# A hybrid decoder block on one core: the norm's row spread through memory, the router's scaling moved, two weight pieces moved behind a store

## The chip, the cores and the metric

The kernel runs on one core of one Trainium2 chip. The metric is the device time of one execution in microseconds (us), here the median of a few runs; lower is better. The engines are named as in the profile: PE (TensorE; PEld are its weight loads), DVE (VectorE), ACT (ScalarE), POOL (GpSimd) and SP (SyncE, here only an issuer of DMAs). SPq, ACTq and POOLq are the instruction streams that issue DMAs.

## The reference

All data is float32: 2048 tokens, width 1024, one layer. Cut to what matters:

```python
hn = rms_norm(x, norm_mix)                    # x * rsqrt(mean(x*x) + eps) * gain
proj = hn @ w_in + b_in                       # q k v o, gates i f (4 heads of 128), conv b c x
h_m = mlstm_chunkwise(q * 128**-0.5, k, v, log_i, log_f)
y_m = sigmoid(o) * h_m
y_c = short_gated_conv(cb, cc, cx, conv_w)    # width 3
x = x + concat([y_m, y_c]) @ w_out
hn2 = rms_norm(x, norm_ffn)
moe = hier_moe(hn2, ...)                      # top-1 of 4 groups, top-2 of its 8 experts, 512 wide
out = rms_norm(x + moe, norm_final)           # silu(hn2 @ w_gate[e]) * (hn2 @ w_up[e]) @ w_down[e]
```

## The kernel before

**Stages.** The tokens pass in four blocks (`NB = 4`) of 512 (`TB`), each of four tiles of 128 (`CT`), in the order of the code; then the 32 experts follow, ordered by the number of tokens that chose them. Each engine has its own instruction stream, written out by hand; semaphores (`S_("name")`) tie the streams together. An engine waits in order: all that stands behind a waiting instruction waits too.

**A block.** PE multiplies the transposed, normed input `hnT` with slices of `w_in`, in "parts" of a Strassen-like scheme (seven half-size products in place of eight), first q and k, then the output gate, then the values v (`v_part`, read by DVE in `v_reads`), and the convolution channels between the four chunks of the mLSTM. DVE forms the sums that such products need (`x_sums`, `ysums`), POOL those of the weights (`weight_sums`). The output projection follows as two halves `p` of seven parts each (`out_part`, in the order 1, 7, 6, 2, 5, 3, 4); DVE adds their results and the residual in `out_reads`. In block 0 the value products are read between 85 and 113 us.

**The norm of the next block.** ACT squares and sums the rows of the next block (`norm_squares`), POOL makes `ssx[:, 2, :]`, 128 partitions x 4 tiles, of 1/rms (`norm_scales`, semaphore `rs_ready`). `hnT` has its tokens along the free axis, so 1/rms is needed as one row of 512 tokens on all 128 partitions. Before, DVE multiplied the identity by the four columns (`norm_diagonals`, line 1941, tile `zz`, seen as `rdiag`), and PE multiplied a matrix of ones by it into the PSUM tile `RB` (`norm_rows`, line 812) between the two halves of the output projection; `norm_scaled` (line 1948) multiplied `hnT` by it. Block 0 has a path of its own at the start, which stays as it is.

**The tail of a block on ACT.** After `norm_squares(b + 1)` ACT issues the store of the first tile of x (`store_residual(0)`, line 1332), squares it (line 1340) and goes on with the other tiles. The stored x is loaded again by SP in quads (line 518) and turned by DVE (`turned_tile`, line 2271) for the router's logits on PE (`router_logits`, line 866), which stand behind part 6 of the second half.

**The router's weights.** `wrt` (8 x 64 columns) is multiplied by the norm's gain on DVE once, in block 0, ahead of the sums of y (line 2549); `ysums(0, (1, 2))` follow (lines 2447 and 2450), and PE's part 6 waits for the second.

**From the blocks to the experts.** The rows `hn2` are stored by ACT, the last 128 of them at line 1448. POOL then gathers each expert's tokens from memory: the first 128 of item 0 (line 1719), the up to 32 further ones of item 0 (`gather_tail(0)`, line 1743), then item 1's. The gather of item 0's first rows doesn't need the last stored rows, the tail gather does. Gate and up weights of an expert come as four pieces of 1 MB into `wo`'s place (`gate_up_piece`, line 634), the down weights as two of 1 MB (`down_piece`, line 638: into `og` and `vx`); `first_weights` issues those of item 0. PE needs piece j from its k tile 2j on (`first_gate_up`, lines 1085 and 1087), then does the further rows (`late_gate_up`, line 1118), turns item 1's rows (line 1063), and multiplies by the down weights (line 1157). DVE meanwhile sorts the experts and makes all the indices in one long chain of small dependent operations (lines 2748 to 2843), in which it also turns item 0's further rows (line 2711) and multiplies item 1's hidden rows (`hidden(1)`, line 2705), for which PE's down products wait.

Of the kernel before, what the change touches and what calls it, by code (L numbers as in the profile page):

```python
# [18 lines left out]
P = 128  # L19
# [14 lines left out]
def build(nc, x, xT_d, w_slots, channel_d, bias_d, w_out, w_router, late_d, gfin_d, w_gu, w_dn, out):  # L34
# [35 lines left out]
    wv_d = nc.dram_tensor("w_v_sums", (4, P, KT // 2 * WC), F32, kind="Internal").ap()  # L70
    yn_d = nc.dram_tensor("attention_rows", (S, DM), F32, kind="Internal").ap()
    row3_d = nc.dram_tensor("gate_rows", (H * TB,), F32, kind="Internal").ap()
    slots_d = nc.dram_tensor("slots", (CAP * NE, 2), F32, kind="Internal").ap()
    over_d = nc.dram_tensor("over_slots", (OVMAX * CAP + P, 2), F32, kind="Internal").ap()

    with ExitStack() as ctx:
# [382 lines left out]
        def v_loaded(b, i):  # L459
# [4 lines left out]
            return S_("second_loaded1"), (2 * b + (1 if i == 2 else 2)) * 16  # L464
        NCONST = 2
        NRC = 15 + 2 * TQ
# [17 lines left out]
        def own_instruction(eng):  # L484

            eng.sem_inc(S_("waits_done"), 1)
# [5 lines left out]
        def _(sp):  # L492
# [148 lines left out]
            def first_weights():  # L641
                sp.wait_ge(S_("yn_ready"), NTILE)
                down_piece(0, 0)
                sp.wait_ge(S_("out_part_done"), out_part_end(NB - 1, 1, 7))
                gate_up_piece(0, 0)
                sp.wait_ge(S_("out_part_done"), out_part_end(NB - 1, 1, 4))
                sp.wait_ge(S_("x_gathered"), 16)
                for j in range(1, NWS):
                    gate_up_piece(0, j)
                sp.wait_ge(S_("x4_gathered"), 16)  # L650
                down_piece(0, 1)
# [45 lines left out]
        def _(pe):  # L697
# [111 lines left out]

            def norm_rows(b):  # L810
                pe.wait_ge(S_("rdiag_ready"), b + 1)
                pe.matmul(RB[:], ones[:], zz[:], start=True, stop=True
                          ).then_inc(S_("norm_rows_done"), 1)
# [4 lines left out]
            def first_gates():  # L818

                for k in range(KT):  # L820
                    pe.wait_ge(S_("xg_ready"), k + 1)
                    if k == 0:
                        pe.wait_ge(S_("w_first_loaded"), 16)
                    if k == KH:
                        w_here(0, 4)
                    for t in range(CT):
                        mm = pe.matmul(FIRST_BANK[t][:, 0:WC], xraw[:, k, t * P:(t + 1) * P], slot_weights(4, k, 0, WC),
                                       start=(k == 0), stop=(k == KT - 1))
                        if k == KT - 1:
                            mm.then_inc(S_("proj_done"), 1)  # L830
                w_here(0, 5)
                for t in range(CT):
                    if t >= 2:
                        pe.wait_ge(S_("bank_emptied"), t - 1)
                    for k in range(KT):
                        mm = pe.matmul(FIRST_BANK[CT + t][:, 0:WG], xraw[:, k, t * P:(t + 1) * P],
                                       slot_weights(5, k, 0, WG), start=(k == 0), stop=(k == KT - 1))
                    mm.then_inc(S_("proj_done"), 1)
                    if t == 0:
                        pe.wait_ge(S_("masks_ready"), 1)  # L840
                        norm_rows(0)

# [17 lines left out]
            def router_logits(g, t):  # L860
                pe.wait_ge(S_("wrt_ready"), 1)
                pe.wait_ge(S_("hn2T_ready"), 2 * g + 2)
# [7 lines left out]
            def router_rows(g):  # L870

                pe.wait_ge(S_("both_halves_ready"), 1)
                pe.wait_ge(S_("lgT_ready"), g + 1)
                pe.matmul(STA[:, 0, P:P + NR], lgT[:], both_halves[:], start=True, stop=True
                          ).then_inc(S_("logits_done"), 1)
# [34 lines left out]
            for b in range(NB):  # L910
# [93 lines left out]
                for p in range(2):  # L1004
                    pe.wait_ge(S_("yT_ready"), b * CT + 2 * (p + 1))
                    if p == 1 and b < NB - 1:
                        norm_rows(b + 1)
                    for i, bank, new in OUT_PARTS:
# [213 lines left out]
        def _(act):  # L1222
# [26 lines left out]
            with act.Fori(0, NB) as b:  # L1249
# [76 lines left out]
                with act.If(b < NB - 1):  # L1326
                    norm_squares(b + 1)
                def store_residual(t):
                    g = b * CT + t
# [142 lines left out]
        def _(pool):  # L1472
# [21 lines left out]
            pool.memset(cmask[:].rearrange("h (c t) -> h c t", c=CT)[:, :, 0:1], 0.0).then_inc(m, 1)  # L1494
            pool.wait_ge(m, 15)
            pool.sem_inc(S_("masks_ready"), 1)
            rc = S_("route_consts")
# [439 lines left out]
        def _(dve):  # L1937
            def norm_diagonals(b):
                dve.wait_ge(S_("rs_ready"), b + 1)
                for t in range(CT):  # L1940
# [3 lines left out]
            def norm_scaled(b, half):  # L1944
                dve.wait_ge(S_("norm_rows_done"), b + 1)
                dve.wait_ge(S_(f"xT_loaded{half}"), 16 * (b + 1))
                for k in range(4 * half, 4 * half + 4):
                    dve.scalar_tensor_tensor(out=hnT[:, k, :], in0=hnT[:, k, :], scalar=gmix[:, k:k + 1], in1=RB[:],
                                             op0=ALU.mult, op1=ALU.mult).then_inc(S_("hnT_ready"), 1)
# [14 lines left out]
            for j in range(4):  # L1964
                dve.wait_ge(S_(XRAW_LOADED[j]), 16)
                for k in (2 * j, 2 * j + 1):
                    dve.tensor_scalar(xraw[:, k, :], xraw[:, k, :], gmix[:, k:k + 1], None, ALU.mult
                                      ).then_inc(S_("xg_ready"), 1)
            dve.wait_ge(S_("masks_ready"), 1)
            norm_diagonals(0)  # L1970
            dve.wait_ge(S_("biases_loaded"), 16)
# [50 lines left out]
            class Route:  # L2022
# [126 lines left out]
                def one_hot(self):  # L2149
                    for j in range(2):  # L2150
# [4 lines left out]
                        if j == 0 and self.T == TL:  # L2155
# [5 lines left out]
            dve.tensor_tensor(both_halves[:], ident[:, 0:NR], ident[:, RW:RW + NR], ALU.add  # L2161
                              ).then_inc(S_("both_halves_ready"), 1)
            dve.wait_ge(S_("route_consts"), NRC)
            dve.scalar_tensor_tensor(out=pad[:, 1:2], in0=jcol[:], scalar=-float(R1), in1=pad[:, 0:1], op0=ALU.mult,
                                     op1=ALU.add).then_inc(S_("pad_step"), 1)
            dve.wait_ge(S_("pad_step"), 1)
            dve.tensor_scalar(pad[:, 1:2], pad[:, 1:2], float(P), None, ALU.add).then_inc(S_("pad_step"), 1)
            dve.wait_ge(S_("pad_step"), 2)
            dve.tensor_scalar(mtail[:, 0:1], pad[:, 1:2], float(S + 1 + P + R2), None, ALU.is_lt
                              ).then_inc(S_("pad_step"), 1)  # L2170
            dve.tensor_scalar(mtail[:, 2:3], pad[:, 1:2], float(S + 1 + P + R3), None, ALU.is_lt
                              ).then_inc(S_("pad_step"), 1)
            dve.tensor_scalar(mtail[:, 3:4], pad[:, 1:2], float(S + 1 + P + R4), None, ALU.is_lt
                              ).then_inc(S_("pad_step"), 1)
            dve.tensor_scalar(mtail[:, 1:2], pad[:, 1:2], -1.0, None, ALU.add).then_inc(S_("pad_step"), 1)
            dve.wait_ge(S_("pad_step"), 6)
            dve.tensor_scalar(mtail[:, 1:2], mtail[:, 1:2], float(TQ), jcol[:, 0:1], ALU.mult, ALU.add
                              ).then_inc(S_("pad_step"), 1)
            dve.wait_ge(S_("pad_step"), 7)

            it = S_("item_step")
            item_steps = [0]

            def then(ins):
                item_steps[0] += 1
                ins.then_inc(it, 1)
                dve.wait_ge(it, item_steps[0])


            def decoded(rows_, code, n_, pad_, after):  # L2190
# [9 lines left out]
            for b in range(NB):  # L2200
# [74 lines left out]
                for r in range(RQ):  # L2275
# [14 lines left out]
                    if b > 0:  # L2290
# [19 lines left out]
                        if r == 13:  # L2310
                            routed.slots()
                            dve.sem_inc(rt, NSTEP - routed.n)

                def v_reads(names):

# [32 lines left out]
                if b < 1:  # L2348
                    dve.tensor_tensor(bvd[:], bvo[:, 0, WC:2 * WC], bvo[:, 0, 0:WC], ALU.subtract
                                      ).then_inc(S_("v_bias_ready"), 1)  # L2350
                dve.wait_ge(S_("v_bias_ready"), 1)
                if b > 0:
                    for s in range(2):
                        for t in range(CT):
                            ps = done(number[("o", (s, t))])
                            if s == 1:
                                dve.tensor_tensor(gt[:, t, :], ps[:, WC:WG], bgt, ALU.add
                                                  ).then_inc(S_("gates_ready"), 1)
                            dve.tensor_tensor(og[:, t, s * WC:(s + 1) * WC], ps[:, 0:WC], bvo[:, 1, s * WC:(s + 1) * WC],
                                              ALU.add).then_inc(E, 1)  # L2360
                v_reads(("p1",))
                gates_later((0, 0), (1, 0), (0, 1))

# [181 lines left out]

                dve.wait_ge(S_("consts_loaded"), 16 * NCONST)
                if b < 1:
                    for k in range(KT):
                        i_ = dve.tensor_scalar(wrt[:, k, :], wrt[:, k, :], gffn_c[:, k:k + 1], None, ALU.mult)
                    i_.then_inc(S_("wrt_ready"), 1)  # L2550
                def out_reads(p, names):
# [61 lines left out]
                out_reads(0, ("u2", "c11", "u4", "c22", "r12"))  # L2613
                if b < NB - 1:
                    norm_diagonals(b + 1)
                out_reads(0, ("c12", "u3", "r21", "r22", "c21"))
# [442 lines left out]
```

## Time and profile before

| | |
|---|---|
| median of 3 runs | 1774.49 us (1774.33 to 1776.5) |
| the profiled execution's time | 1775.47 us |
| its span in the profile | 1773.7 us |
| PE busy | 1753.0 us, 99% of the span |
| PEld busy | 1403.6 us, 79% |
| DVE busy | 926.6 us, 52% |
| ACT busy | 234.4 us, 13% |
| POOL busy | 676.3 us, 38% |
| mean granted clock of PE | 0.998 of full speed |

The busy times are of the one profiled execution; its time is 1.8 us above its span. A fp32 matmul stands in the trace as two records. Records of PE overlap in the trace, so the pace of a run of them is the distance of their starts. A row with a bracket names the idle time of the engine ahead of the instruction and what ended it; an "x8" behind a row means that so many instructions are merged in it. Times in the timeline count from the start of the span.

### The profile page before, as it was taken

How to read it: one execution, taken by the hardware profiler on the slowest of the kernel's cores; microseconds unless marked ns; L12 is line 12 of the kernel's file. 1: busy time of each engine (PE TensorE's matmuls, PEld its weight loads, DVE VectorE, ACT ScalarE, POOL GpSimd, SP SyncE). 2: the span in 40 equal slices, each digit the busy share in tenths (PEclk: the TensorE clock that was granted, in tenths of full speed). 3: DMA queues.
4: the chain of work that ended last, by engine and by line, in shares of the span. 5: the costliest groups of instructions: out<-in, count | busy, mean ns of one | idle time of the engine just before them, and what ended most of it. 6: DMA issues, size and time to landing. Idle time of an engine off the chain costs nothing. (4 is left out here: it accounts for less than half of the span.)

```text
span 1773.7 us, 27565 instructions
## 1 busy us (share of the span) xinstructions
PE 1753.0 (99%) x10077; PEld 1403.6 (79%) x10077; DVE 926.6 (52%) x1897; ACT 234.4 (13%) x618; POOL 676.3 (38%) x755
## 2 busy tenths in 40 slices
PE   9999999999999999999999999999999999999997
PEld 8889658889578887588885678887888888888876
DVE  5556785377773677763776683433433233233332
ACT  2021110211101211102210210011110011100111
POOL 5933212044221235030341124444445455554552
PEclk9999999999999999999999999999999999999999
DMA  7553742234732327422334488898999998999984
GB/s 295 222 200 99 273 166 86 96 135 152 258 107 84 131 96 258 163 102 96 129 113 150 167 320 334 336 340 333 347 345 333 353 355 324 348 340 332 346 330 179
DMA packets 101373, 406.81 MB, mean 229 GB/s; under 512 B 20982, under 2 KB 35630, under 8 KB 68464
## 3 DMA queue, kind: packets, MB, share of 16 engines
q1 hardware_dynamic: 57488, 316.78, 48.3%
q0 software_dynamic: 26880, 58.91, 9.3%
q10 hardware_dynamic: 16880, 29.43, 4.5%
q8 instruction: 82, 1.34, 0.3%
q14 instruction: 43, 0.35, 0.1%
HBM read 366.59 MB, written 64.53 MB: 243 GB/s over the span
## 5 line engine op out<-in xcount | busy, mean ns | idle before, releaser
L1135 PE MATMUL ps_proj<-hnT,wo 128*128 128x128 f32 (+4 forms) x992 | 199.9, 283 | 0.0
L1137 PE MATMUL ps_proj<-hnT,wo 128*128 128x128 f32 (+4 forms) x992 | 197.9, 281 | 0.0
L1726 POOL DMA_INDIRECT xin<-hn_rows,idx_quad x116 | 117.3, 1011 | 125.7 <-DVE hnT L2711 46.4
L1135 PEld LDWEIGHTS ps_proj<-hnT,wo 128*128 128x128 f32 x992 | 153.9, 191 | 13.6 <-issue 13.6
L1137 PEld LDWEIGHTS ps_proj<-hnT,wo 128*128 128x128 f32 x992 | 153.2, 191 | 0.0
L743 PE MATMUL ps_proj<-hnT,ww 128*128 128x256 f32 x640 | 151.9, 380 | 0.0
L743 PEld LDWEIGHTS ps_proj<-hnT,ww 128*128 128x128 f32 x640 | 120.1, 191 | 16.4 <-issue 1.4
L1565 POOL TENSOR_TENSOR xres<-ww 128x512 f32<-128x512 f32 x12 | 15.2, 1268 | 291.2 <-DMA ww<-in_w_slots 279.3
L2942 DVE SCALAR_TENSOR_TENSOR hn<-xin,rsy,ww 128x1024 f32<-128x1024 f32 x30 | 38.5, 1285 | 136.1 <-POOL rsy L1784 136.1
L1135 PE MATMUL ps_scores<-hnT,wo 128*128 128x128 f32 (+4 forms) x496 | 99.1, 282 | 0.0
L1135 PE MATMUL ps_rows<-hnT,wo 128*128 128x128 f32 (+4 forms) x496 | 99.0, 281 | 0.0
L1137 PE MATMUL ps_scores<-hnT,wo 128*128 128x128 f32 (+4 forms) x496 | 99.0, 281 | 0.0
L1137 PE MATMUL ps_rows<-hnT,wo 128*128 128x128 f32 (+4 forms) x496 | 98.9, 281 | 0.0
L772 PE MATMUL ps_proj<-wo,yT 128*128 128x512 f32 x192 | 88.8, 600 | 0.0
L2705 DVE TENSOR_TENSOR kT<-qT,ps_proj 128x128 f32<-128x128 f32 (+4 forms) x62 | 15.6, 293 | 134.8 <-ACT qT L1420 134.5
L784 PE MATMUL ps_proj<-ww,hnT 128*128 128x256 f32 (+1 forms) x384 | 84.7, 383 | 0.0
L784 PEld LDWEIGHTS ps_proj<-ww,hnT 128*128 128x128 f32 x384 | 73.1, 190 | 11.0
L1137 PEld LDWEIGHTS ps_scores<-hnT,wo 128*128 128x128 f32 x496 | 76.7, 192 | 0.0
L1135 PEld LDWEIGHTS ps_rows<-hnT,wo 128*128 128x128 f32 x496 | 76.6, 191 | 0.0
L1137 PEld LDWEIGHTS ps_rows<-hnT,wo 128*128 128x128 f32 x496 | 76.6, 191 | 0.0
L1135 PEld LDWEIGHTS ps_scores<-hnT,wo 128*128 128x128 f32 x496 | 76.5, 191 | 0.0
L743 PE MATMUL ps_proj<-xin,ww 128*128 128x256 f32 x320 | 76.4, 381 | 0.0
(523 smaller groups left out, 3493.9 us busy)
## 6 DMA issues: line engine op xcount, KB each, us to landing
wo<-in_w_gu SPq DMA_DIRECT2D x128, 1024.0 KB, 7.7
ww<-in_w_slots SPq DMA_DIRECT2D x43, 1024.0 KB, 4.9
og<-in_w_dn SPq DMA_DIRECT2D x32, 1024.0 KB, 5.3
vx<-in_w_dn SPq DMA_DIRECT2D x32, 1024.0 KB
xin<-in_x SPq DMA_DIRECT2D x16, 512.0 KB, 5.3
ww<-w_v_sums SPq DMA_DIRECT2D x16, 512.0 KB, 3.4
xres<-in_x SPq DMA_DIRECT2D x16, 512.0 KB, 6.1
x_rows<-x ACTq DMA_DIRECT2D x16, 512.0 KB, 3.6
```

The source lines that it names most:

```text
L743: mm = pe.matmul(place, w_(k), x_[:, k, :], start=(new and k == 0), stop=(k == KH - 1), skip_group_check=True)
L772: mm = pe.matmul(place, y_[:, k, :], w_[:, k, :], start=(new and k == 0), stop=(k == KH - 1), skip_group_check=True)
L784: mm = pe.matmul(PROJ[:, n % 2, 0:w], hnT[:, k, t * P:(t + 1) * P], slot_weights(slot, k, 0, w), start=(k == 0), stop=(k == KT - 1))
L1135: pe.matmul(GU[m][:, 0:n_], wo[:, kt, m * P:(m + 1) * P], xT[:, kt, 0:n_], start=(kt == 0), stop=(kt == KT - 1), skip_group_check=True)
L1137: mm = pe.matmul(GU[m][:, CAP:CAP + n_], wo[:, kt, FF + m * P:FF + (m + 1) * P], xT[:, kt, 0:n_], start=False, stop=(kt == KT - 1), skip_g ...
L1565: pool.tensor_tensor(wsum(s, 1, first), a21, a22, ALU.add).then_inc(ready, 1)
L1726: pool.indirect_dma_start(xg[:, t * TC:(t + 1) * TC], None, hn2_d.rearrange("s (j c) -> (s j) c", j=TQ), bass.IndirectOffsetOnAxis(ap=idx_ ...
L2705: i_ = dve.tensor_tensor(hT[:, m, 0:n_], sgt[:, m, 0:n_], src[:, CAP:CAP + n_], ALU.mult)
L2942: dve.scalar_tensor_tensor(out=fo, in0=yr[:], scalar=rsy[:, 1, 0:1], in1=gfin, op0=ALU.mult, op1=ALU.mult).then_inc(S_("out_rows_ready"), 1)
```

## The change

Three things are changed, and some semaphores with them.

1. In blocks 1 to 3 the row of 1/rms no longer comes from PE. ACT waits for POOL's scales, stores the 128 x 4 words in token order in memory (`norm_scales`, 2 KB), waits until they have landed, and loads the row into `zz` on all 128 partitions (256 KB); `norm_scaled` reads `zz`. The products of `norm_rows` and DVE's `norm_diagonals` stay for block 0 alone.
2. The eight scalings of `wrt` stand among DVE's reads of the value products of block 0 (three ahead of the first, five behind it), not ahead of the sums of y.
3. The last gate/up piece and the second down piece of item 0 are issued when the last rows' store has landed. Before, piece 3 was issued when the first gather had landed, the down piece when the tail gather had. What SP issues behind them (`gfin`) moves with them.

Four semaphores are dropped or merged: `masks_ready` (now `mask_step` at 15), `wrt_ready` and `both_halves_ready` (now `router_consts` at 3), `pad_step` and `v_bias_ready` (now the counter of `then`, which waits after each instruction).

```diff
+    scale_d = nc.dram_tensor("norm_scales", (S,), F32, kind="Internal").ap()
...
-                for j in range(1, NWS):
-                    gate_up_piece(0, j)
-                sp.wait_ge(S_("x4_gathered"), 16)
+                gate_up_piece(0, 1)
+                gate_up_piece(0, 2)
+                sp.wait_ge(S_("hn2_stored1"), 16 * NTILE // 2)
+                gate_up_piece(0, 3)
                 down_piece(0, 1)
...
             def router_logits(g, t):
-                pe.wait_ge(S_("wrt_ready"), 1)
+                pe.wait_ge(S_("router_consts"), 3)
...
                 for p in range(2):
                     pe.wait_ge(S_("yT_ready"), b * CT + 2 * (p + 1))
-                    if p == 1 and b < NB - 1:
-                        norm_rows(b + 1)
...
                 with act.If(b < NB - 1):
                     norm_squares(b + 1)
+                    act.wait_ge(S_("rs_ready"), b + 2)
+                    own_instruction(act)
+                    row = scale_d[bass.ds(b * TB, TB)]
+                    act.dma_start(row.rearrange("(t p) -> p t", p=P), ssx[:, 2, :],
+                                  allow_slow_non_contiguous=True).then_inc(S_("scales_stored"), 16)
+                    act.wait_ge(S_("scales_stored"), 16 * (b + 1))
+                    own_instruction(act)
+                    act.dma_start(zz[:], row.partition_broadcast(P)).then_inc(S_("scales_spread"), 16)
...
             def norm_scaled(b, half):
-                dve.wait_ge(S_("norm_rows_done"), b + 1)
+                dve.wait_ge(S_("scales_spread"), 16 * b)
                 dve.wait_ge(S_(f"xT_loaded{half}"), 16 * (b + 1))
                 for k in range(4 * half, 4 * half + 4):
-                    dve.scalar_tensor_tensor(out=hnT[:, k, :], in0=hnT[:, k, :], scalar=gmix[:, k:k + 1], in1=RB[:],
+                    dve.scalar_tensor_tensor(out=hnT[:, k, :], in0=hnT[:, k, :], scalar=gmix[:, k:k + 1], in1=zz[:],
...
+                def router_weights(ks):
+                    if b < 1:
+                        dve.wait_ge(S_("consts_loaded"), 16 * NCONST)
+                        for k in ks:
+                            i_ = dve.tensor_scalar(wrt[:, k, :], wrt[:, k, :], gffn_c[:, k:k + 1], None, ALU.mult)
+                        i_.then_inc(S_("router_consts"), 1)
...
+                router_weights(range(3))
                 v_reads(("p1",))
+                router_weights(range(3, KT))
                 gates_later((0, 0), (1, 0), (0, 1))
...
-                dve.wait_ge(S_("consts_loaded"), 16 * NCONST)
-                if b < 1:
-                    for k in range(KT):
-                        i_ = dve.tensor_scalar(wrt[:, k, :], wrt[:, k, :], gffn_c[:, k:k + 1], None, ALU.mult)
-                    i_.then_inc(S_("wrt_ready"), 1)
...
                 out_reads(0, ("u2", "c11", "u4", "c22", "r12"))
-                if b < NB - 1:
-                    norm_diagonals(b + 1)
                 out_reads(0, ("c12", "u3", "r21", "r22", "c21"))
```

## Rows read from the trace of the kernel before

**Rows 1.** Waits of PE: who waited for whom, us in total, times, longest.
```profile
PE ps_proj L772 <- issue: 2.3, 1, 2.3
```

**Rows 2.** Timeline of PE, tail of block 0: start us, us, engine, line, instruction.
```profile
227.66 1.02 PE L812 MATMUL ps_rows<-zz,ones 128*128 128x512 f32 x2
...
228.52 3.60 PE L772 MATMUL ps_proj<-wo,yT 128*128 128x512 f32 x8
```

**Rows 3.** Timeline in block 0, and one sum of block 1.
```profile
96.57 0.69 DVE L2332 TENSOR_TENSOR vx<-ps_proj,vx 128x512 f32<-128x512 f32 x1 [7.02 <-PE ps_proj L805]
...
203.25 5.75 DVE L2549 TENSOR_SCALAR wrt<-wrt,by_channel 128x64 f32<-128x64 f32 x8
...
204.48 3.60 PE L772 MATMUL ps_state<-wo,hn2T 128*128 128x512 f32 x8
...
209.62 0.69 DVE L2450 TENSOR_TENSOR uu<-uu,yT 128x512 f32<-128x512 f32 x1
...
210.42 3.67 PE L772 MATMUL ps_proj<-kT,uu 128*128 128x512 f32 x8 [2.34 <-issue]
...
455.20 1.66 DVE L2450 TENSOR_TENSOR uu<-uu,yT 128x512 f32<-128x512 f32 x1
```

**Rows 4.** Timeline, router's tile and logits in the tail of block 1.
```profile
482.78 2.10 DVE L2271 STREAM_TRANSPOSE hn2T<-attn 128x512 f32<-128x512 f32 x2 [0.23 <-DMA attn<-x_rows]
...
485.45 1.09 PE L866 MATMUL ps_state<-hn2T,wrt 128*64 128x128 f32 x16
```

**Rows 5.** Timeline of POOL and ACT's queue, tail of block 1.
```profile
461.60 1.05 POOL L1535 TENSOR_TENSOR ssx<-ssx,mhalf 128x4 f32<-128x4 f32 x1
...
471.89 0.38 ACTq L1332 DMA_DIRECT2D x_rows<-x  x1
```

**Rows 6.** DMAs of attention_rows, and the slot stores of L1682.
```profile
DMA to landing us min/median/max: 1.8/2.1/9.0
...
DMA to landing us min/median/max: 4.2/6.0/6.9
```

**Rows 7.** Timeline, from the blocks to the experts.
```profile
1018.24 0.35 ACTq L1448 DMA_DIRECT2D hn_rows<-hn  x1
...
1019.84 0.44 PE L1085 MATMUL ps_proj<-hnT,wo 128*128 128x128 f32 x2
...
1023.78 1.04 POOL L1743 DMA_INDIRECT xin<-hn_rows,idx  x1 [16.38 <-issue]
...
1026.71 0.63 DVE L2711 STREAM_TRANSPOSE hnT<-xin 128x256 f32<-128x256 f32 x1 [0.26 <-DMA xin<-hn_rows,idx]
...
1027.40 1.92 POOL L1719 DMA_INDIRECT xin<-hn_rows,idx_second  x1 [2.59 <-DVEq L2745]
...
1028.92 3.66 PE L1118 MATMUL ps_scores<-wo,hnT 128*32 128x256 f32 x64
...
1035.47 1.95 PE L1063 MATMUL ps_num<-ident,xin 128*128 128x128 f32 x8 [2.89 <-DMA xin<-hn_rows,idx_second]
...
1060.46 0.48 DVE L2705 TENSOR_TENSOR kT<-qT,ps_proj 128x128 f32<-128x128 f32 x2
...
1062.97 1.45 PE L1157 MATMUL ps_state<-og,kT 128*128 128x512 f32 x3
```

**Rows 8.** Windows: us, busy of PE, PEld, DVE, ACT, POOL; PEclk, DMA share, GB/s.
```profile
1034.00:1039.00 5.00, 3.53 (x11) 2.58 (x12) 4.62 (x13) 1.19 (x2) 0.00 (x0) 0.66 1.03 410
...
208.00:210.00 2.00, 0.08 (x1) 0.00 (x0) 1.97 (x4) 1.68 (x5) 0.78 (x1) 1.00 1.02 399
```

**Rows 9.** DMA landings: L1346's stores; L1743 at 1044, then all of it; gate/up pieces.
```profile
DMA to landing us min/median/max: 2.6/4.7/6.8
...
DMA to landing us min/median/max: 4.8/4.8/4.8
...
DMA to landing us min/median/max: 2.7/6.7/8.2
...
DMA to landing us min/median/max: 4.8/7.7/11.6
```

More of the change, by code:

```diff
@@ L464, in v_loaded @@
             return S_("second_loaded1"), (2 * b + (1 if i == 2 else 2)) * 16
-        NCONST = 2
+        NCONST, MASK_STEPS = 2, 15
         NRC = 15 + 2 * TQ
@@ L808, in v_part, with norm_rows @@
                 mm.then_inc(S_("v_part_done"), 1)
-            def norm_rows(b):
-                pe.wait_ge(S_("rdiag_ready"), b + 1)
+            def norm_rows():
+                pe.wait_ge(S_("rdiag_ready"), 1)
                 pe.matmul(RB[:], ones[:], zz[:], start=True, stop=True
@@ L839, in first_gates @@
                     if t == 0:
-                        pe.wait_ge(S_("masks_ready"), 1)
-                        norm_rows(0)
+                        pe.wait_ge(S_("mask_step"), MASK_STEPS)
+                        norm_rows()
             def warm_up(n):
@@ L870, in router_rows @@
             def router_rows(g):
-                pe.wait_ge(S_("both_halves_ready"), 1)
                 pe.wait_ge(S_("lgT_ready"), g + 1)
@@ L1494, in _ @@
             pool.memset(cmask[:].rearrange("h (c t) -> h c t", c=CT)[:, :, 0:1], 0.0).then_inc(m, 1)
-            pool.wait_ge(m, 15)
-            pool.sem_inc(S_("masks_ready"), 1)
+            pool.wait_ge(m, MASK_STEPS)
             rc = S_("route_consts")
@@ L1937, in _, with norm_diagonals @@
         def _(dve):
-            def norm_diagonals(b):
-                dve.wait_ge(S_("rs_ready"), b + 1)
+            def norm_diagonals():
+                dve.wait_ge(S_("rs_ready"), 1)
                 for t in range(CT):
@@ L1968, in _ @@
                                       ).then_inc(S_("xg_ready"), 1)
-            dve.wait_ge(S_("masks_ready"), 1)
-            norm_diagonals(0)
+            dve.wait_ge(S_("mask_step"), MASK_STEPS)
+            norm_diagonals()
             dve.wait_ge(S_("biases_loaded"), 16)
@@ L2161, in _ @@
             dve.tensor_tensor(both_halves[:], ident[:, 0:NR], ident[:, RW:RW + NR], ALU.add
[L2162 to L2179, printed above, removed]
+                              ).then_inc(S_("router_consts"), 1)
             it = S_("item_step")
@@ L2187, in then @@
                 dve.wait_ge(it, item_steps[0])
+            dve.wait_ge(S_("route_consts"), NRC)
+            then(dve.scalar_tensor_tensor(out=pad[:, 1:2], in0=jcol[:], scalar=-float(R1), in1=pad[:, 0:1], op0=ALU.mult,
+                                          op1=ALU.add))
+            then(dve.tensor_scalar(pad[:, 1:2], pad[:, 1:2], float(P), None, ALU.add))
+            then(dve.tensor_scalar(mtail[:, 0:1], pad[:, 1:2], float(S + 1 + P + R2), None, ALU.is_lt))
+            then(dve.tensor_scalar(mtail[:, 2:3], pad[:, 1:2], float(S + 1 + P + R3), None, ALU.is_lt))
+            then(dve.tensor_scalar(mtail[:, 3:4], pad[:, 1:2], float(S + 1 + P + R4), None, ALU.is_lt))
+            then(dve.tensor_scalar(mtail[:, 1:2], pad[:, 1:2], -1.0, None, ALU.add))
+            then(dve.tensor_scalar(mtail[:, 1:2], mtail[:, 1:2], float(TQ), jcol[:, 0:1], ALU.mult, ALU.add))
             def decoded(rows_, code, n_, pad_, after):
@@ L2348, in _ @@
                 if b < 1:
-                    dve.tensor_tensor(bvd[:], bvo[:, 0, WC:2 * WC], bvo[:, 0, 0:WC], ALU.subtract
-                                      ).then_inc(S_("v_bias_ready"), 1)
-                dve.wait_ge(S_("v_bias_ready"), 1)
+                    then(dve.tensor_tensor(bvd[:], bvo[:, 0, WC:2 * WC], bvo[:, 0, 0:WC], ALU.subtract))
                 if b > 0:
```

## The prediction

> **What bounds the kernel now.** I began with the page's busy times: TensorE (PE) is busy 99% of the span (table above), so a microsecond is won only by taking work off PE or by closing a gap in PE's own stream. Then the list of what PE waited for: its longest gap is for the gather of the second expert's rows [rows 7], the next, 2.3 us, has no releaser named ("issue") [rows 1]. Then the timeline at the places that the diff touches. The reader is to see three things. In a block's tail PE multiplies one 128x512 product after another at 0.43 us a record, and `norm_rows` sits in that stream without a wait: 227.66 to 228.52, 0.86 us [rows 2]. In block 0 the unnamed gap stands behind `wrt`'s scaling: DVE works on it from 203.25 for 5.75 us, only then makes the sums of y, the last needed one ends at 210.31, and PE, whose product of 204.48 lasts 8 records or 3.43 us, is free at 207.91 and starts at 210.42 [rows 3]. And at the change from blocks to experts PE stands 2.89 us until 1035.47 [rows 7].
>
> **`norm_rows` in blocks 1 to 3.** Three times two records: 3 x 0.86 = 2.58 us off PE, and 0.9 us off DVE (four 0.28 us scalings), which has waits there. What is late next is the router: in each of the three tails the logits follow PE's third part, and their turned tile is ready only just before. In block 1's tail it ends at 484.88 and PE begins at 485.45 [rows 4]. DVE's chain to that tile starts from the last sum of the first half, which PE's saving doesn't make earlier. PE would be there at 484.59; with the 0.11 us that a hand-over takes in [rows 3] it waits until 484.99, 0.40 us. The same rows of the other two tails give 0.24 and 0.14. Left of 2.58: 1.8 us. The new copy of the row (0.25 MB) runs on the queue of the stores that feed this tile; below nothing it can't come, and it costs up to 0.6 us a block if it delays them by its own length. I take 0.1 in all: 1.7 us, ends 0.0 and 2.6.
>
> **The row through memory.** ACT now waits for `rs_ready`, stores 128x4 single words, waits for the landing, issues the spread and goes on to `store_residual(0)`, `squares_of`, `store_rows`, for whom POOL, the quad loads on SP, DVE's tile and PE's logits wait. In block 1 the scales are ready at 462.65, so the store goes at about 463.1; ACT's next job comes at 471.89 [rows 5]: 8.8 us are free (9.7 in block 0, 9.2 in block 2, from the same rows there). No row shows words stored singly. Nearest are `attention_rows`, 2.1 us in the median and 9.0 at the longest, and the 8-byte slot stores of POOL, 4.2 to 6.9 [rows 6]. I take 6: hidden, 0 us; at 9.0 it would cost 0.2 us a block. The spread (0.25 MB) then lands by about 472, ten microseconds before the tile of 482.78 [rows 4], ahead of which DVE runs half of `norm_scaled`. That this reads `zz` rather than PSUM I put at nothing; if each of the four products became 0.1 us longer, PE would wait 0.4 us more a block, which the lower end of 0.0 above includes. The Trainium skill ("DMA: Bandwidth & Descriptors", Specifications) says that transfers under 512 B are done by read-modify-write, which speaks against this store; it gives no price for it, and no run here yet shows one.
>
> **`wrt`'s scaling.** The same eight instructions go where DVE waits for `v` products in block 0 (its second read there follows 7.02 us of idleness [rows 3]), at up to 5.75 us with POOL beside them as here; hidden. In the tail the two sums start at 203.3. With POOL at work such a sum lasts 1.66 us in block 1 [rows 3], so both end at about 206.6, before PE's 207.91. The gap closes: 210.42 - 207.91 = 2.5 us, ends 2.2 (0.3 late) and 2.6. What is next behind it on DVE, `p1`, then comes at 206.6 and is needed a part later, at 211.3; if the early place of the scaling were not covered, its 5.75 us would hold up `v`'s reads by that much.
>
> **The last gate/up piece and the down piece.** Before, pieces 1 to 3 go when the first gather has landed, and the down piece and `gfin` when the tail gather has, just before 1026.71, beside the second gather of 1027.40 [rows 7]. Now piece 3 and the down piece wait for the landing of the last rows' store (issued 1018.24), and `gfin` follows them at once; all three stand in SP's queue behind that wait, and `expert_weights` of item 1 behind them, which needs the items' numbers of 1026.5 anyway. Step by step:
> - The store meets 2 MB less traffic: 2.6 us, the least of its kind [rows 9], so landed at 1020.9.
> - Piece 3 goes at 1021.0 and lands after 4.8 (the least) to 7.7 us (the median) [rows 9]; I take 5.2, 1026.2. PE's k tile 3 begins at 1019.84 and five tiles last until 1028.92, 1.82 each: tile 6 is due at 1025.3. PE waits 0.9 us (0.5 to 3.4), and its arrival at the second transposes moves from 1032.58 to 1033.5.
> - The second gather, still issued at 1027.40, no longer meets the down piece and `gfin`: instead of 7.9 us some 5, so 1032.5, ahead of PE. The transposes start at 1033.5, 2.0 us sooner.
> - In that gap the granted clock falls: 0.66 in the mean over 1034 to 1039 [rows 8], the lower of the two levels (1.2 GHz) for some 3 us, against 1.00 throughout. Of (1 - 0.66) x 5 = 1.7 us some fall into the gap itself; I take 1.4 that come back. At 1038 PE would be 3.4 us ahead.
> - But DVE's chain runs without a gap from 1026.71 to `hidden(1)` at 1060.46, first half ready at 1061.3, and PE's down product starts at 1062.97 [rows 7]. Only 1.7 us of the 3.4 can pass. And DVE's chain hangs on the tail gather, for which it waited 0.26. That gather can now go at 1022.4, but beside 2.7 MB. Uncontended it took 2.7 us; 4.8 at 1044, behind the third item's rows and beside the next weights; the median of all is 6.7 [rows 9]. Before it landed at 1023.78 + 2.7 = 1026.5; with 2.7, 4.8, 6.7 it becomes 1025.1, 1027.2, 1029.1: chain 0.26 earlier, 0.7 or 2.6 later. I take 4.8, the row nearest in place and size: 1.7 - 0.7 = **1.0 us**, ends 1.9 and -0.9.
>
> **Sum.** 1.7 + 2.5 + 1.0 = 5.2 us. The other edits (`mask_step`, and waits between seven tiny operations of DVE at the start) are hidden behind PE's products; without that cover they cost some 0.3 us. The profiled execution took 1775.47, 0.98 above the median: 1770.3 for it, 1769.3 for the median.
>
> **Rivals.**
> - *The expert stage gives nothing back or takes.* The tail gather needs 6.7 us, or PE's new gap ahead of the first down product of item 1 (3.4 - 1.0 = 2.4 us) lets the clock fall again as the one of 2.89 did. For: the gather shares the engines with 2.7 MB. Against: the gap of 2.5 us at 208 left the clock at 1.00 [rows 8]. Stage -0.9: 1771.2.
> - *The gap at 208 has another cause,* a loaded sum of weights for instance. For: no releaser is named. Against: PE starts 0.11 us after DVE's sum. 1769.3 + 2.5 = 1771.8.
> - *DVE isn't the limit at 1060* and all 3.4 pass: 1766.9. Against: no idle time stands in DVE's rows.
> - *Slower: ACT is held by the word store.* Its place is the wait for `scales_stored`; from a landing of 8.8 us on, each further microsecond is one of PE's three times. It eats the whole gain at 8.8 + 5.2/3 = 10.5 us; at 12 it costs 9.6: 1778.9. For: 512 separate words, with no row for such. Against: the longest 8-byte store took 6.9 [rows 6].
>
> **How the numbers follow.** Forecast 0.60 (own range 1767.3 to 1770.9), expert stage 0.20, another cause 0.07, all passes 0.07, word store 0.06. A measurement tells 0.2%, 3.5 us, from no change: the border is 1770.9. Faster: 0.53 of the forecast, the 0.07, and a share of 0.06 of the expert case: 0.66. Slower: most of the word store, 0.05. Same: the rest, 0.29. The range 1766.0 to 1773.2 holds the ends of the three sums taken singly (2.6 less for the first two, 0.9 for the clock and the gather together with a late tile) and leaves out the slower case.
>
> **What would show it.** `norm_rows` gone from three tails with PE waiting 0.1 to 0.4 us for the turned tile; no gap of PE near 208; the word store landing within 8 us and `x_rows<-x` issued at the same distance behind its sum; piece 3 landing after 1025.3 with a short gap of PE there, no half clock at 1035, and a new gap ahead of item 1's down product, ended by `hidden(1)`. Wrong it is if ACT's `x_rows` issue comes late, if the tail gather takes over 5 us, or if the clock falls in a new gap.

## The result

The changed kernel takes **1796.51 us** in the median of four runs (1795.46 to 1798.52), the kernel before beside it 1774.41 (1774.07 to 1776.5): ratio 1.0119, 95% interval 1.0105 to 1.0133. It is 1.2% slower; I had forecast 1769.3 us and put the slower side at 0.05. By the ratio that is 21.1 us, by the medians 22.1. Differences in us behind a ratio are worked out from the ratio below, too.

### The profile page after: what moved, and what is told of

It is laid out like the page before. It is cut to its first block and busy times, and to the rows that moved or that the text cites. A ratio compares the mean times of both kernels' runs of the same rounds, so it can differ in the third digit from the quotient of the medians.

```text
span 1793.7 us, 27536 instructions
## 1 busy us (share of the span) xinstructions
PE 1756.8 (98%) x10071; PEld 1404.1 (78%) x10071; DVE 924.0 (52%) x1885; ACT 234.2 (13%) x618; POOL 678.9 (38%) x755
```

## The profile after

The profiled execution has a span of 1793.7 us, against 1773.7, so 20.0 us are to be found. I first set the starts of the output projection of the four blocks side by side: 201.05, 450.04, 696.57, 943.91 in the kernel before, 201.59, 455.12, 708.10, 960.65 after. From one to the next the blocks grew by 4.5, 6.5 and 5.2 us, so the loss sits in each of the tails 0 to 2, 16.2 us in all. From the last of these starts to the first transposes of the experts nothing changed (66.66 and 66.73), and some 3 us went in the expert stage.

The waits of PE (who waited for whom, us in total, times, longest):

```profile
PE ps_state L868 <- issue: 17.2, 3, 6.1
PE ps_state L1156 <- issue: 3.5, 1, 3.5
PE ps_num L1062 <- DMA xin<-hn_rows,idx: 1.4, 1, 1.4
PE ps_proj L1084 <- DMA wo<-in_w_gu: 0.7, 1, 0.7
```

L868 is the router's logits: three waits of 5.4 to 6.1 us that the kernel before didn't have [rows 4]. The gap of 2.3 us [rows 1] is gone, and so is that of the second transposes. In its place stand 3.5 us ahead of a down product (L1156).

The timeline of the tail of block 0, the rows of ACT's and SP's queues, POOL, DVE and PE that matter:

```profile
212.29 1.38 POOL L1541 TENSOR_TENSOR ssx<-ssx,mhalf 128x4 f32<-128x4 f32 x1
213.90 0.44 ACTq L1330 DMA_DIRECT2D norm_scales<-ssx  x1
...
222.39 0.69 DVE L2600 TENSOR_TENSOR x<-ps_proj,x 128x512 f32<-128x512 f32 x1 [1.15 <-PE ps_proj L774]
...
226.72 0.37 ACTq L1334 DMA_DIRECT2D zz<-norm_scales  x1
227.40 0.37 ACTq L1339 DMA_DIRECT2D x_rows<-x  x1
...
233.50 4.56 SPq L519 DMA_DIRECT2D attn<-x_rows  x8
...
239.97 2.07 DVE L2268 STREAM_TRANSPOSE hn2T<-attn 128x512 f32<-128x512 f32 x2 [3.25 <-DMA attn<-x_rows]
...
242.14 1.97 PE L868 MATMUL ps_state<-hn2T,wrt 128*64 128x128 f32 x16 [6.05 <-issue]
```

The words are issued at 213.90 and the spread only at 226.72: 12.8 us. DVE's sum for `x_rows` ends at 223.1, but the store goes at 227.40, 4.3 us late. It lands at 233.4, and SP's quads start at 233.50; DVE's tile waits for them, and PE for the tile. After six microseconds of idleness PE comes back at the lower clock: the sixteen records of L868 last 1.97 us, 1.09 before [rows 4]. The window of the logits (columns as in [rows 8]; the clock stands after POOL) has a granted clock of 0.50, where the kernel before has 1.00:

```profile
242.00:244.00 2.00, 1.86 (x16) 1.60 (x16) 2.00 (x5) 0.00 (x0) 0.00 (x0) 0.50 0.03 8
```

The three tails add up so: 17.2 us of waits, less 2.6 for `norm_rows` and 2.3 for the gap that closed, leave 12.3 of the 16.2; the other 3.9 us are my estimate of what the lower clock behind the waits costs.

The landings of the word store, the three of them:

```profile
DMA to landing us min/median/max: 11.1/11.2/12.7
```

I had taken 6 us, from stores that took 2.1 and 6.0 in the median [rows 6].

The expert stage, where [rows 7] showed the kernel before:

```profile
1039.39 1.04 POOL L1749 DMA_INDIRECT xin<-hn_rows,idx  x1 [15.27 <-DVEq L2754]
1044.29 1.00 POOL L1725 DMA_INDIRECT xin<-hn_rows,idx_second  x1 [3.86 <-DVEq L2742]
...
1042.91 0.49 PE L1084 MATMUL ps_proj<-hnT,wo 128*128 128x128 f32 x2 [0.69 <-DMA wo<-in_w_gu]
1050.27 1.16 PE L1062 MATMUL ps_num<-ident,xin 128*128 128x128 f32 x8
...
1080.19 3.75 PE L1156 MATMUL ps_state<-og,kT 128*128 128x512 f32 x4 [3.52 <-issue]
```

and a window over that down product:

```profile
1080.00:1090.00 10.00, 9.81 (x18) 4.35 (x19) 5.50 (x15) 0.00 (x0) 4.12 (x5) 0.71 0.35 121
```

Counted from the first transposes (1010.57 before, 1027.38 after), the second ones start 22.9 us on instead of 24.9: the 2.0 us that I had forecast. DVE's row of `tail_turned`, at 1045.93 behind a wait of 2.60 us for the tail gather, comes 2.4 us later than before. The down product of item 1 starts at 52.8 instead of 52.4 and its four groups end at 62.7 instead of 59.4: 0.4 us by the late start, 2.8 by the clock, at 0.71 in the window above.

## The experiments: each part by itself

Three kernels undo two parts each: the row through memory alone, `wrt`'s scaling alone, the pieces alone. The last two are edits of the kernel before.

> The kernel before with the row through memory alone: router weights scaled in the tail and the weights' pieces as before. Theory (ACT is held by the word store, 11 to 13 us from issue to landing, then its stores come late): the three tails lost 4.55 + 2.5 (the gap that closed there), 6.45 and 6.11 us between the two profiles, so +19.6 us, 1794 (1791 to 1797), with x_rows issued 4 us late in block 0. Rival (the row is cheap, and the loss comes from the other two parts or from all three together): under +10 us.

Measured: 1794.42 against 1775.52, ratio 1.0114 (1.0097 to 1.0132), **+20.2 us**. The row is the loss. (The 6.11 in my expectation was misread: the third tail grew by 5.2 us, which makes that sum 18.7. The range holds what was measured either way.)

> The kernel before with the scaling of the router's weights moved among the value products, nothing else. Theory: the gap of 2.5 us at 208 closes and nothing else moves: 1771.9 (1771 to 1773). Rival (the scaling isn't covered at its new place, which would also explain the 0.54 us by which the changed kernel starts its first output projection late): the gap closes but 0.5 us or more goes ahead of it: 1772.5 to 1774.

Measured: 1773.92 against 1775.52, ratio 0.9992 (0.9983 to 1.0001), -1.4 us (-3.0 to +0.2). The gap closes, as forecast; the gain is under the 2.5 us that I expected, though the interval holds 2.5 as well as nothing. The gap isn't always as wide as in my one profile. With the scaling in the tail the same eight instructions lasted 5.75 us in the kernel before [rows 3], and in the timelines of the row alone and of the pieces alone

```profile
203.58 4.69 DVE L2543 TENSOR_SCALAR wrt<-wrt,by_channel 128x64 f32<-128x64 f32 x8
```
```profile
202.79 2.46 DVE L2550 TENSOR_SCALAR wrt<-wrt,by_channel 128x64 f32<-128x64 f32 x8
```

and the gap behind them is 2.34, 2.23 and at most 0.5 us in these three. In the other four traces with the scaling in the tail (of the experiments on the pieces, below) the eight last 5.55, 3.44, 4.67 and 5.58 us and the gap is 2.15, 0.98, 2.22 and 2.17 us. So the wide gap is the common case, five of seven. Where the eight are quick, POOL's sums of weights beside them are slow: four of 1.36 to 1.93 us beside the 2.46, four of 1.26 or 1.27 us beside the 5.75. Why one or the other gives way was not found. A late start of the first projection (the rival) isn't there: over the traces it lies between 200.6 and 201.7 with the scaling at either place.

> The kernel before with the last gate/up piece and the down piece behind the last rows' store, nothing else. Theory (the tail gather becomes slow beside 2.7 MB, DVE's chain to hidden(1) runs some 2.3 us late and PE has a gap of 3.5 us ahead of the second down product, in which its clock falls): +3.3 us, 1777.7 (1776 to 1779). Rival (the loss of that stage in the changed kernel came with the late blocks ahead of it, the move itself gives the 1.0 us that I forecast): 1773.4.

Measured: 1778.14 against 1775.52, ratio 1.0015 (1.0006 to 1.0025), **+2.7 us** (1.1 to 4.4). Theory held: tail gather issued 1019.36, its row on DVE at 1025.96 behind a wait of 2.66 us, a gap of 3.57 us ahead of the down product and slow records behind it.

## The experiments: why the row costs

**Smaller number of pieces.** Each partition stores its four scales as 16 bytes, and DVE reads the row with a stride:

```
-act.dma_start(row.rearrange("(t p) -> p t", p=P), ssx[:, 2, :], ...)
+act.dma_start(row.rearrange("(p t) -> p t", p=P), ssx[:, 2, :], ...)
-... in1=zz[:]
+... in1=zz[:].rearrange("a (p t) -> a t p", p=P)
```

> The changed kernel, but each partition stores its four scales as one piece of 16 bytes (128 pieces instead of 512), and VectorE reads the row with a stride. Theory (the landing is set by the number of single pieces): it falls from 11 to 13 us to 2 to 5, ACT is no longer held past its slack of 8.8 us, and the tails lose at most the queueing of the spread ahead of x_rows (about 2 us each): 1777 to 1783. Rival (the landing is a fixed latency, or it waits behind the weight loads): still 10 us or more, 1794 to 1798.

Measured: 1777.64 against 1775.52, ratio 1.0016 (1.0003 to 1.0029), +2.8 us, and these landings:

```profile
DMA to landing us min/median/max: 4.4/4.7/6.5
```

Of the changed kernel's 21.1 us 18.3 are back, so it is the way in which the words are stored; whether by holding ACT or otherwise isn't told yet. The strided read isn't free: a product of `norm_scaled` lasts 1130 ns in the mean and not 741, and PE waits up to 1.6 us for the tile.

**Who waits.** So far the hold of ACT could be the whole cost. Next, SP waits for the landing and issues the spread:

```
-act.wait_ge(S_("scales_stored"), 16 * (b + 1)); act.dma_start(zz[:], ...)
+sp.wait_ge(S_("scales_stored"), 16 * (b + 1));  sp.dma_start(zz[:], ...)   # ahead of load_x2_quad
```

> The changed kernel (all three parts, 512 single words), but SyncE waits for the landing of the word store and issues the spread, ahead of its quad loads; ACT only issues the store and goes on. Theory (it is ACT's wait that costs, not the words themselves): x_rows goes at the same distance behind its sum as in the kernel before, the words land about 226 in block 0, SP's quads are due at 228.6, and of the row's 20 us nearly all comes back: before plus 0 us (-2 to +4), most of which is the 2.7 us of the weights' pieces. Rival (single words hold up the DMA engines, so x_rows lands late though it is issued on time): before plus 10 us or more.

Measured: 1792.56 against 1775.31, ratio 1.0097 (1.0081 to 1.0114), **+17.2 us**. My theory fell. ACT is free, and `x_rows` goes right behind its sum (timeline of ACT's and SP's queues in the tail of block 0):

```profile
213.96 0.44 ACTq L1334 DMA_DIRECT2D norm_scales<-ssx  x1
...
221.26 4.18 SPq L509 DMA_DIRECT2D xres<-in_x  x2
...
223.08 0.40 ACTq L1340 DMA_DIRECT2D x_rows<-x  x1
...
231.31 5.06 SPq L519 DMA_DIRECT2D attn<-x_rows  x8
```

but it lands 8.1 us later. The view of the transfers says why. First its packets by queue from 217 to 219 (queue, packets, MB, share of 16 engines), then from 221 to 223, then the issues of 210 to 230 with their median landings:

```profile
q1 hardware_dynamic: 39, 0.19, 23.1%
q10 hardware_dynamic: 528, 0.00, 14.8%
...
q1 hardware_dynamic: 25, 0.10, 158.9%
...
xres<-in_x SPq DMA_DIRECT2D x2, 512.0 KB, 8.4
x_rows<-x ACTq DMA_DIRECT2D x2, 512.0 KB, 8.0
norm_scales<-ssx ACTq DMA_DIRECT2D x1, 2.0 KB, 13.2
```

All words have gone out by 219, but their landing is reported at 227. In between, SP's load of `xres`, another queue, reading other memory, gets 25 packets through in 2 us, and they last some 2 us each (an estimate: 158.9% of 16 engines x 2 us, over 25). In the kernel before the same stretch has

```profile
xres<-in_x SPq DMA_DIRECT2D x2, 512.0 KB, 4.2
x_rows<-x ACTq DMA_DIRECT2D x2, 512.0 KB, 4.1
```

So transfers of other queues take twice as long while the words are under way. (The Trainium skill, "DMA: Bandwidth & Descriptors", Back-pressure in remote DMA, says for transfers between cores that stalled writes stall the other queues of the same engine. What this trace shows for stores of one core to its own memory looks alike; that it is the same thing is not shown.) The run doesn't yet clear the spread: it lands late too, and DVE waits 3.5 us for it here.

**The place of the spread.**

```
-wait scales_stored; spread; store_residual(0); squares_of(0)
+wait scales_stored; store_residual(0); squares_of(0); spread
```

> The changed kernel, ACT still waits for the words' landing, but issues the spread only behind store_residual(0) and squares_of(0). Theory (of the 6.5 us lost in a tail some 2 us are the 256 KB of the spread ahead of x_rows on its queue, the rest is the hold itself): x_rows(0) lands in 4 us and not 6, three tails give 2 us each: the changed kernel less 6 us, 1790 (1788 to 1793). Rival (the spread's place is of no account, the hold is all): 1795 or more.

Measured: 1795.94 against 1775.31, ratio 1.0116 (1.0101 to 1.0132), +20.6 us. The changed kernel had 1.0119, so the place of the spread is of no account; my theory fell.

**Words that nobody reads.** `norm_rows` on PE is put back; the store alone stays:

```
+norm_diagonals(b + 1) ... norm_rows(b + 1) ... in1=RB[:]      # as in the kernel before
-act.wait_ge(S_("scales_stored"), 16 * (b + 1)); act.dma_start(zz[:], ...)
+act.wait_ge(S_("scales_stored"), 16 * b)                      # in the middle of the next block
```

> norm_rows on TensorE and VectorE's scalings as in the kernel before, router weights' scaling moved, weights' pieces as before; only the word store is left of the row's way through memory: ACT issues it in each of the three tails, nobody waits for it there and nobody reads it. Theory (after the run in which SyncE did the waiting: the 512 words hold up the transfers of all queues until they have landed, whoever waits): each tail still loses 5 us or so, before plus 13 to 18 us (1788 to 1793). Rival (what costs is a wait or the spread, not the words): before plus 3 us or less.

Measured: 1788.55 against 1775.39, ratio 1.0073 (1.0051 to 1.0095), **+13.0 us**, with 9.3 us of waits at the logits and these landings:

```profile
DMA to landing us min/median/max: 11.1/11.9/13.5
```

No wait and no reader is needed. The two kernels that follow differ from this one only in where the words go; against them the words side by side cost 13.1 and 13.9 us. The remaining 6 to 7 of the row's 20.2 us, and the 2.6 us that the row saves (below), some 9 us together, I put down to ACT's hold, which comes from the late landing, and to the spread. That is an estimate by subtraction between kernels; no run shows it by itself.

**The same words further apart.** One constant differs: word n goes to `n * 128` or `n * 16` instead of n.

> The same with the words stored 512 bytes apart in memory. Theory A (words side by side are what is slow, each rewriting the memory line of its neighbour): the landing falls from 12 us to under 6 and the loss to 3 us or less. Theory B (the number of single words counts, wherever they go): landing and time as with the words side by side.

> As the run with unread words, stored 64 bytes apart instead of 512. If only words in the same 64 bytes hinder each other: landing under 6 us and time as with 512 bytes. If the unit is larger (512 bytes hold eight of them): landing between 5 and 12 us, before plus 3 to 13 us.

Measured at 512 bytes: 1775.14 against 1775.39, ratio 0.9999 (0.9990 to 1.0008). At 64 bytes: 1775.13 against 1775.37, ratio 0.9995 (0.9986 to 1.0004). Landings of the one and of the other:

```profile
DMA to landing us min/median/max: 4.9/4.9/4.9
```
```profile
DMA to landing us min/median/max: 4.8/5.0/5.6
```

As many words, the same store in every other way, and no loss. So it isn't the number of words, but how close they lie. In the trace at 512 bytes, too, the words' queue has 528 packets, and the loads of `xres` behind them, from 221 to 223, go as

```profile
q1 hardware_dynamic: 34, 0.14, 35.7%
```

which is 0.34 us for a packet, where it was 2 us with the words side by side (the same estimate as above). Side by side sixteen words share 64 bytes. Of the 16-byte pieces above four did, and they landed in 4.7 us. Distances between 4 and 64 bytes were not tried for words. Neither of the two kernels reads its words back, so what a spread from words 64 bytes apart costs is not known.

## The experiments: the pieces

Two kernels move one piece alone behind the landing of the last rows' store, `sp.wait_ge(S_("hn2_stored1"), ...)`, and leave the other as in the kernel before.

> The kernel before with only the down piece (and gfin behind it) issued behind the landing of the last rows' store, gate/up piece 3 at once as before. Theory (1 MB beside the tail gather makes it late; the piece is then out of the second gather's way): VectorE's chain starts 1 to 2 us late, PE has no wait at the second transposes but one of 2 to 4 us ahead of the second down product, with half a clock behind it: before plus 1 to 3 us. Rival (the tail gather is late only because piece 3 goes with it): 1 to 2 us under the kernel before.

> The kernel before with only gate/up piece 3 behind the landing of the last rows' store, the down piece behind the tail gather as before. Theory (piece 3 beside the tail gather makes that gather late too): tail gather 1 to 2 us late, the second gather still meets the down piece, so PE still waits there, and the two waits come on top of each other: before plus 1 to 3 us. Rival (the store and the early gather gain what piece 3 loses): within 1 us of the kernel before.

The down piece alone: 1779.46 against 1775.37, ratio 1.0024 (1.0014 to 1.0033), **+4.3 us**, more than the 1 to 3 expected. Piece 3 alone: 1775.62, ratio 1.0004 (0.9995 to 1.0013): nothing; the rival held. So it is the down piece, with `gfin` behind it, that makes the tail gather slow. That both together cost less (+2.7) than the down piece alone fits the traces: without piece 3 ahead of it the last rows' store lands after 2.6 us and not 4.6, and the tail gather is issued 11.9 us behind the first transposes and not 13.2. DVE's row with the wait, and PE's down product of item 1, of the down piece alone:

```profile
1030.78 0.64 DVE L2711 STREAM_TRANSPOSE hnT<-xin 128x256 f32<-128x256 f32 x1 [3.79 <-DMA xin<-hn_rows,idx]
...
1065.00 3.75 PE L1157 MATMUL ps_state<-og,kT 128*128 128x512 f32 x4 [3.53 <-issue]
1068.55 2.88 PE L1157 MATMUL ps_state<-vx,kT 128*128 128x512 f32 x4
```

The transfers stand nearly still from 1020 to 1028 in the kernel before (109 and 47 GB/s). Two kernels put the down piece there: one right behind piece 3, without its wait, and one at the moment of the last rows' store (`sp.wait_ge(S_("hn2_ready"), NTILE)`).

> The kernel before with the down piece (and gfin behind it) issued right behind gate/up piece 3, without the wait for the tail gather. In the kernel before the transfers stand nearly still from 1020 to 1028 (109 and 47 GB/s). Theory (the pause is what costs: its traffic is what the second gather meets afterwards): the wait of 2.89 us ahead of the second transposes goes, so does its half clock, and VectorE's chain to hidden(1) is the limit again, 1.7 us under the kernel before (0.5 to 2.5). Rival (the piece delays the last rows' store and the tail gather, and with them VectorE's chain): 0 to 2 us over it, with a gap ahead of the second down product.

> The kernel before, but the down piece is issued when the last rows are computed, at the moment of their store, and gfin still waits for the tail gather. Theory (the transfers stand nearly still from 1020 to 1028; a down piece that goes then, behind pieces 1 to 3 and beside the store, meets neither gather): the wait of 2.89 us and its half clock go, the store lands up to 1 us later, VectorE's chain is the limit: 0.7 to 1.7 us under the kernel before. Rival (the store shares the engines with 1 MB and lands late, both gathers with it, as in the run with the piece at once): 1 to 3 us over it.

Measured: 1777.50 against 1775.31, ratio 1.0017 (1.0007 to 1.0027), and 1777.92 against 1775.39, ratio 1.0017 (1.0008 to 1.0027), **+3.0 us** each. The rival held both times: the store of the last rows (4.6 us before) now takes

```profile
DMA to landing us min/median/max: 8.5/8.5/8.5
```
```profile
DMA to landing us min/median/max: 8.1/8.1/8.1
```

(landings of that one store in the one and in the other) and the tail gather is issued at 1027.49 and 1026.24 instead of 1023.78. None of the five placings of these pieces gave a gain. The pause in the transfers is the latency of a chain (store, gather, turned rows), and the down piece, put into it, lengthens the chain each time; piece 3 there cost nothing that could be told.

## The experiments: a version without the words

Pieces of 16 bytes; ACT, idle between `squares_of(0)` and `store_residual(1)`, puts the row in token order into the PSUM bank that `norm_rows` wrote; `wrt`'s scaling moved; pieces as before:

```
+act.wait_ge(S_("scales_spread"), 16 * (b + 1))
+act.activation(RB (t p), zz (p t), ACT.Copy)
```

> Scales stored as 128 pieces of 16 bytes; ACT, idle between squares_of(0) and store_residual(1), puts the row in token order into the PSUM bank that norm_rows wrote, so that VectorE's products are those of the kernel before; router weights' scaling moved; weights' pieces as in the kernel before. Theory (the parts add up: row 1.7 us won once nothing is held, scaling 1.6): 3.3 us under the kernel before (1.5 to 5). Rival (PE's 0.86 us a tail only turn into a wait for the turned tile, or what is saved there is lost in the clock): 1.6 us under it, that of the scaling alone, or less.

> The version with pieces of 16 bytes, ACT's reordering and the moved scaling, with the down piece issued as in the run beside it. If the parts add up: 1.4 us under the kernel before as that version measured, and 0.7 to 1.7 more: 2 to 3 us under it, 1772.5. If the rival of the run beside it holds, no better than the version itself.

Measured: 1773.07 against 1775.31, ratio 0.9992 (0.9981 to 1.0003), -1.4 us; with the down piece at the rows' store 1774.23 against 1775.39, ratio 0.9996 (0.9988 to 1.0005), -0.7 us: the parts that were to add up to 2 to 3 us don't, as the down piece loses here too. The second stood beside the same placing without the other parts (1777.92): **3.7 us less**. The traces agree: from the first output projection to the last it is 738.3 and 738.0 us, against 740.9 with the scaling alone and 740.4 and 740.7 with the words 512 and 64 bytes apart: 2.1 to 2.9 us for three tails, about the whole of 3 x 0.86. By the two ratios the first version is 1.3% faster than the changed kernel; against the kernel before its gain is within the noise.

## Why the prediction was wrong

- **The word store, taken at 6 us and hidden: wrong, and the step that failed.** It lands after 11.1 to 12.7 us, and while it is under way 512 KB transfers of other queues take some 8 us instead of 4; that alone costs 13 us. The rival "ACT is held by the word store" had the place and a symptom, the late `x_rows`, but at a landing of 12 us it gave 1778.9, far below what was measured: with ACT free 17.2 us are still lost, of which the pieces are 2.7. I priced the store by its own landing and asked who waits for it; what it does to the transfers beside it I left at nothing. The nearest rows [rows 6] were stores of another kind (8 bytes a piece, or whole rows), and no row showed single words. (The Trainium skill, "DMA: Bandwidth & Descriptors", Specifications, spoke against the store, by its read-modify-write below 512 bytes. The measurement agrees with the direction only: single words 64 bytes apart are as far below 512 bytes and landed in 5.0 us.)
- **The tails amplify it.** I had one microsecond of PE for each of lateness in each tail; the clock adds to that, 1.97 us for 1.09 at the logits and some 3.9 us over the three tails.
- **`norm_rows`, 1.7 us: right in kind, rather more.** Without words side by side the tails give some 2.5 us. At the logits PE waits 1.2 us in two of them, against 1.0 in one with the scaling alone, so less was to be subtracted than my 0.8. A read from `zz` costs what one from PSUM does: 741 ns both.
- **`wrt`'s scaling, 2.5 us: right mechanism.** The gap closed in every trace. It measures 1.4 us (-0.2 to 3.0); the two kernels with the words 512 and 64 bytes apart, which have the same move, came out 0.2 and 0.9 us under the kernel before. I took one profiled execution's gap for every execution's: it is 2.15 us or more in five of seven and small in two, and in the trace of the scaling alone 1.0 us comes back as a wait at the logits. The rival with another cause fell.
- **The weights' pieces, 1.0 us: wrong, +2.7.** Step by step: piece 3 came 0.7 us late (forecast 0.9), the transposes 2.0 us sooner (2.0), but the tail gather took 6.5 us from issue to DVE's row and not 4.8, nearly my bad end of 6.7, which put the down product 0.4 us late. And the clock fell in the new gap of 3.5 us. I had it as a rival, with the price of 1.9 us between the two cases; the clock alone took 2.8. I left it out of the sum because a gap of 2.5 us had gone by at full clock [rows 8].
- **The sum.** 20.2 for the row, -1.4 and +2.7 make 21.5; measured 21.1 by the ratio, 22.1 by the medians. The upper end of my range, 1773.2, is 3.9 us above the forecast, as the three ends give it (1.7, 0.3 and 1.9); the 2.6 and 0.9 written beside it don't add up to that.

## What to carry to other kernels

A small strided store isn't priced by its bytes or its own landing: look at the window of all queues around it, and at how close its pieces lie in memory (here 4 bytes apart was slow, 64 bytes apart was not, and nothing between was tried for words). Pieces of 16 bytes a partition, with the reordering left to an idle engine, showed no such loss; nor did words 64 bytes apart, but nobody read those. A transfer moved into a pause must be checked against a latency chain of small transfers that may run through the pause; and a gap that is merely moved must be priced with the clock behind it.

## What was not expected of the hardware

- 512 words of 4 bytes side by side are out in some 2 us and reported landed 8 us later; while they are under way loads and stores of other queues take 8 us instead of 4. 64 bytes apart the same words land in 5.0 us and cost nothing. That neighbours in the same 64 bytes are rewritten one after the other would fit this, but only the distance was tried, not the mechanism.
- The same eight small VectorE instructions lasted between 2.46 and 5.75 us at the same place in seven executions, with POOL's sums beside them slow where they were quick. Open.
